# Fourteen expert rows of each head fetched and multiplied beside the next head's routing, with six score units a head

## The reference

```python
def peer_ffn(xn, w_query, sub_keys, expert_u, expert_v):
    q = (xt @ w_query).reshape(NT, PEER_HEADS, 2, D_KEY // 2)
    s = jnp.einsum('nhpd,pkd->nhpk', q, sub_keys)
    v1, i1 = lax.top_k(s[:, :, 0], PEER_TOPK)
    v2, i2 = lax.top_k(s[:, :, 1], PEER_TOPK)
    cand = (v1[..., :, None] + v2[..., None, :]).reshape(NT, PEER_HEADS, PEER_TOPK * PEER_TOPK)
    best, ci = lax.top_k(cand, PEER_TOPK)
    e1 = jnp.take_along_axis(i1, ci // PEER_TOPK, axis=-1)
    e2 = jnp.take_along_axis(i2, ci % PEER_TOPK, axis=-1)
    idx = e1 * N_KEYS + e2
    gate = jax.nn.softmax(best, axis=-1)
    ...
        act = jax.nn.gelu(jnp.einsum('cd,ced->ce', xc, expert_u[ic]), approximate=False)
        return jnp.einsum('ce,ced->cd', (gc * act).astype(xc.dtype), expert_v[ic])
```

## Time and profile before

| what | us |
| --- | --- |
| median of 3 runs | 4150.55 |
| lowest and highest | 4140.8, 4151.94 |
| the profiled execution's own time | 4146.39 |
| its span in the trace | 4144.7 |

### The profile page before, as it was taken

One profiled execution on the slowest core, in us unless ns is written; L12 is line 12 of the kernel. 1 busy time (PEld: TensorE's weight loads), 2 busy tenths in 40 slices (PEclk: granted clock), 3 DMA queues, 4 the chain that ended last, 5 costly groups with the idle time before them and its releaser, 6 DMA issues.

```text
span 4144.7 us, 68987 instructions
## 1 busy us (share of the span) xinstructions
PE 3987.2 (96%) x27233; PEld 3554.8 (86%) x27233; DVE 2572.6 (62%) x3495; ACT 1408.9 (34%) x1701; POOL 2311.4 (56%) x930
## 2 busy tenths in 40 slices
PE   7999999999999999989999889999999999999997
PEld 5777777777878787879999789999999999999997
DVE  4343344444455553167775677888738888888785
ACT  4323233333232221133333555555423223333223
POOL 4333233332333444444545457777768889999784
PEclk9999999999999999999999999999999999999998
DMA  3222222222132344233334579999989999999892
GB/s 125 90 85 80 90 75 89 86 85 93 70 117 87 130 143 145 98 130 136 125 124 149 209 281 391 398 398 410 386 321 395 373 383 398 397 390 400 313 383 102
DMA packets 258400, 899.46 MB, mean 217 GB/s; under 512 B 107672, under 2 KB 140696, under 8 KB 162736
## 3 DMA queue, kind: packets, MB, share of 16 engines
q1 hardware_dynamic: 175984, 482.50, 32.4%
q0 software_dynamic: 46080, 335.56, 19.7%
q10 hardware_dynamic: 36160, 78.85, 4.9%
HBM read 828.10 MB, written 68.71 MB: 216 GB/s over the span
## 4 chain that ended last, share of the span: by engine, by line
PE 66%; POOL 11%; issue 10%; DMA 6%; DVE 3%; ACT 3%; SPq 1%; ACTq 0%; POOLq 0%; DVEq 0%
PE ps L403 15%; PE ps L405 14%; PE ps L404 14%; PE ps L1990 5%; POOL wl L394 5%; PE ps L1992 5%; PE ps L1991 5%; DMA raw<-stream 5%; POOL wl L398 4%; PE ps L1679 2%; ACT wh L381 1%; POOL rowb L672 1%; ACT wh L390 1%; POOL act L678 1%; PE ps L1939 1%
## 5 line engine op out<-in xcount | busy, mean ns | idle before, releaser
L398 POOL TENSOR_TENSOR wl<-raw,wh 128x2048 fp32r<-128x2048 f32 x268 | 1245.3, 4647 | 1610.6 <-ACT wh L381 1610.5
L403 PE MATMUL ps<-xh,wh 128*128 128x352 f32 (+1 forms) x3904 | 1438.3, 368 | 37.4 <-DVE xl L1162 18.9
L405 PE MATMUL ps<-xh,wl 128*128 128x352 f32 (+1 forms) x3904 | 1403.8, 360 | 0.0
L404 PE MATMUL ps<-xl,wh 128*128 128x352 f32 (+1 forms) x3904 | 1402.3, 359 | 0.0
L403 PEld LDWEIGHTS ps<-xh,wh 128*128 128x128 f32 x3904 | 743.1, 190 | 136.8 <-issue 40.4
L405 PEld LDWEIGHTS ps<-xh,wl 128*128 128x128 f32 x3904 | 742.0, 190 | 83.0
L404 PEld LDWEIGHTS ps<-xl,wh 128*128 128x128 f32 x3904 | 743.1, 190 | 80.8 <-issue 7.7
L381 ACT ACTIVATE wh<-raw 128x2048 fp32r<-128x2048 f32 x270 | 516.8, 1914 | 859.1 <-PE ps L405 722.4
L1990 PE MATMUL ps<-gah,wh 128*128 128x352 f32 x2048 | 667.7, 326 | 33.5 <-POOL wl L394 22.7
L1992 PE MATMUL ps<-gah,wl 128*128 128x352 f32 x2048 | 662.5, 324 | 0.0
L1991 PE MATMUL ps<-gal,wh 128*128 128x352 f32 x2048 | 660.3, 322 | 0.0
(11 more groups left out here) (335 smaller groups left out, 4151.2 us busy)
## 6 DMA issues: line engine op xcount, KB each, us to landing
raw<-stream SPq DMA_DIRECT2D x396, 1024.0 KB, 5.1
gelu_scratch<-preb ACTq DMA_DIRECT2D x128, 176.0 KB, 6.0
gates_scratch<-stage ACTq DMA_DIRECT2D x22, 1024.0 KB
gt<-gates_scratch SPq DMA_DIRECT2D x32, 704.0 KB, 12.8
act<-gelu_scratch SPq DMA_DIRECT2D x32, 704.0 KB, 17.6
mergegate_scratch<-sgb ACTq DMA_DIRECT2D x32, 256.0 KB, 2.0
sgm<-mergegate_scratch SPq DMA_DIRECT2D x32, 256.0 KB, 2.7
h_in<-x_t SPq DMA_DIRECT2D x4, 1024.0 KB, 8.9
```

The lines of the kernel that those rows point to most:

```text
L398: pool.tensor_tensor(wl[s][:, :], raw[s][:, :], wh[s][:, :].bitcast(F32), ALU.subtract).then_inc(w_lo, 1)
L403: pe.matmul(dst, w_h, h[:, kx, lo:], start=start, stop=False)
L404: pe.matmul(dst, w_h, l[:, kx, lo:], start=False, stop=False)
L405: return pe.matmul(dst, w_l, h[:, kx, lo:], start=False, stop=stop)
```

## The change

SC_HEAD goes from 4 to 6, so 16 score units move from the gates' stage to the heads. Gates are then built in 28 units of two groups and 32 of one, 60 in all. Queries and key products all go through bank 7, so PE's order in a head is now query 0, score 0, query 1, score 1, keys 0, score 2, keys 1, scores 3 to 5. That leaves banks 0 to 3 for `xg` from the first head on: `turn` moves to head 0, and its input `xd` is computed ahead of the heads. The expert numbers of a head are computed as soon as its first token group has them (`sets_ready`). Of each of heads 0 to 6, fourteen rows are fetched by POOL in the next head's eight units, two behind each of seven of them, in four buffers, and used by DVE: six at the end of the head's own selection, four behind the next head's first-key selection, four behind its second-key selection. 30 rows of the first set stay in the gates' stage, behind unit 28. Of the second set 12 rows instead of 7 come before the border. ACT's exponential moves behind the second query unit. DVE's loop over heads is unrolled.

```diff
-SC_HEAD, SC_TAIL, SC_EGT, OH = 4, 6, 2, 4
+SC_HEAD, SC_TAIL, SC_EGT, OH = 6, 6, 2, 4
+SCORE_PLACE = (1, 3, 4, 5, 6, 7)
...
-GATES_TWO = 12
+GATES_TWO = 28
...
-fetches(0, 12, range(3, GATES_TWO), 0)
-fetches(12, SLOTS - 12, range(GATES_TWO, F_GATES + R_TURNED - 1), 0)
-fetches(SLOTS, 7, range(F_GATES + R_TURNED, J_BACK), F_GATES + R_TURNED + 1)
...
+EARLY = 14
+EARLY_ALL = EARLY * (HEADS - 1)
+EARLY_AT = {1: (0, 1), 2: (2, 3), 3: (4, 5), 4: (6, 7), 5: (8, 9), 6: (10, 11), 7: (12, 13)}
+EARLY_LAST, EARLY_KEYS, EARLY_VALUES = range(0, 6), range(6, 10), range(10, EARLY)
...
+MORE = 12
+FETCHED_AT.update({n: -1 for n in range(EARLY_ALL)})
+fetches(EARLY_ALL, SLOTS - EARLY_ALL, range(GATES_TWO, F_GATES + R_TURNED - 1), 0)
+fetches(SLOTS, MORE, range(F_GATES + R_TURNED, J_BACK), F_GATES + R_TURNED + 1)
...
+    homes = range(1, ROWS) if n < EARLY_ALL else range(ROWS_LOW if J_BACK <= FETCHED_AT[n] < J_HIGH else ROWS)
...
@@ gpsimd @@
+            for h in range(HEADS):
+                for c in range(PER_HEAD):
+                    split_lo(pool, U_QUERY + PER_HEAD * h + c, c % 2)
+                    for i in EARLY_AT.get(c, ()) if h else ():
+                        if i == 0:
+                            pool.wait_ge(sets_ready, h + 1)
+                        fetch(EARLY * (h - 1) + i)
...
@@ scalar, act_route @@
                 for c in range(2):
-                    act.wait_ge(w_used, n + c + 1)
-                    split_hi(act, n + c + 2, c)
+                    act.wait_ge(w_used, n + 2 * c + 1)
+                    split_hi(act, n + 2 * c + 2, 0)
                     if not first:
                         act.wait_ge(key_scores, 2 * h + c - 1)
-                    act.activation(qsb[:, c, :], bank(c), ACT.Copy).then_inc(q_saved, 1)
-                    if c == 0 and not first:
+                    act.activation(qsb[:, c, :], bank(7), ACT.Copy).then_inc(q_saved, 1)
+                    if c == 1 and not first:
                         act_softmax(h - 1)
+                    score(c)
...
@@ vector @@
+            dve.tensor_tensor(xd, xh[:, :, 0:P].bitcast(F32), xl[:, :, 0:P].bitcast(F32), ALU.add).then_inc(sets_ready, 1)
+            for h in range(HEADS):
...
+                    for i in (EARLY_VALUES if c else EARLY_KEYS) if h else ():
+                        use(EARLY * (h - 1) + i)
...
+                    if tt == 0:
+                        cut = slice(TOPK * h, TOPK * h + TOPK)
+                        own(dve, dve.scalar_tensor_tensor(idx[:, cut], EG[:, 0, 0, cut], float(NKEYS), EG[:, 1, 0, cut], ALU.mult, ALU.add), sets_ready, h + 2)
                 dve.wait_ge(ex_ready, h + 1)
...
+                for i in EARLY_LAST if h < HEADS - 1 else ():
+                    use(EARLY * h + i)
...
@@ tensor, head @@
+                if not first:
+                    pe.wait_ge(ssb_saved, 2 * h)
+                    unit(pe, n, 0, bank(7))
+                    score(0)
+                pe.wait_ge(q_saved, 2 * h + 1)
+                unit(pe, n + 2, 0, bank(7))
+                score(1)
+                if first:
+                    turn(1)
+                for c in range(2):
                     key_products(h, c)
-                    ahead(SC_HEAD * h + c, c, n + c, first)
-                for c in range(2, SC_HEAD):
-                    ahead(SC_HEAD * h + c, c % 2, n + c)
+                    score(2 + c)
+                for i in range(4, SC_HEAD):
+                    score(i)
```

More of the change, by code:

```diff
@@ L1415, in top16, with use @@
                 step(dve.max_index(idx[:, 8:16], vals[:, 8:16], rep))
-            with dve.Fori(0, HEADS) as h:
-                step.enter(h, 0, STEPS_ROUTE)
+            xg = ps[:, 0:4, :].rearrange("p b n -> p (b n)")
+            def use(n):
+                b = row_buffer(n)
+                dve.wait_ge(row_in[ROW_AT[n]], 16 * ROW_BEFORE[n] + 16)
+                if n < ALL:
+                    dve.scalar_tensor_tensor(b, b, 1.0, xg, ALU.mult, ALU.mult, accum_out=dots[:, slot(n):slot(n) + 1]).then_inc(row_used, 1)
+                else:
+                    dve.wait_ge(row_used, n)
+                    dve.scalar_tensor_tensor(xg, b, coef[:, slot(n):slot(n) + 1], xg, ALU.mult, ALU.add).then_inc(row_used, 1)
+            step(dve.tensor_copy(iota_route, iota128[:, :]))
+            for c in range(4):
+                dve.wait_ge(h_moved[c], 48)
+            dve.tensor_tensor(xd, xh[:, :, 0:P].bitcast(F32), xl[:, :, 0:P].bitcast(F32), ALU.add).then_inc(sets_ready, 1)
+            for h in range(HEADS):
                 for c in range(2):
@@ L1614, in first_units @@
                     for s in range(2):
-                        last = products(pe, bank(dst + s), s, k, P, xh, xl, k, k == 0, k == KT - 1)
+                        dst, lo = into[s]
+                        last = products(pe, dst, s, k, P, xh, xl, k, k == 0, k == KT - 1, lo)
                         if k == KT - 1:
@@ L1889, in key_products @@
             def key_products(h, c):
-                pe.wait_ge(q_saved, 2 * h + c + 1)
+                pe.wait_ge(q_saved, 2 * h + 2)
+                if c:
+                    pe.wait_ge(ssb_saved, 2 * h + 1)
                 for tt in range(TT):
-                    last = pe.matmul(bank(2 + c)[:, P * tt:P * tt + P], qsb[:, c, P * tt:P * tt + P], keys[:, c, :], start=True, stop=True)
+                    last = pe.matmul(bank(7)[:, P * tt:P * tt + P], qsb[:, c, P * tt:P * tt + P], keys[:, c, :], start=True, stop=True)
@@ L1893, in key_products, with turn, ahead @@
                 last.then_inc(key_scores, 1)
-            first_units(U_QUERY, 0, 1)
+            def turn(value):
+                pe.wait_ge(sets_ready, value)
+                for k in range(KT):
+                    last = pe.transpose(bank(k // 4)[:, P * (k % 4):P * (k % 4) + P], xd[:, k, :], ident[:, :])
+                last.then_inc(xg_ready, 1)
+            first_units(U_QUERY, ((bank(7), 0), (bank(4)[:, 0:N], G)), 1)
             pe.wait_ge(routing_in, 16)
-            def ahead(e, s, n, first=False):
+            def ahead(e, s, n, w=None, first=False):
@@ L1900, in ahead, with head @@
                 if not first:
                     pe.wait_ge(pre_ready, e - 1)
-                unit(pe, n, s, bank(4 + s)[:, 0:N], lo=G)
-            def head_scores(h, first=False):
-                n = U_QUERY + PER_HEAD * h + 2
+                unit(pe, n, s if w is None else w, bank(4 + s)[:, 0:N], lo=G)
+            def head(h, first=False):
+                n = U_QUERY + PER_HEAD * h
+                score = lambda i: ahead(SC_HEAD * h + i, i % 2, n + SCORE_PLACE[i], SCORE_PLACE[i] % 2, first and i < 2)
+                if not first:
[7 more added lines that the diff above has]
+                    turn(1)
@@ L1906, in head_scores @@
                 for c in range(2):
-                    if not first:
-                        pe.wait_ge(ssb_saved, 2 * h + c - 1)
                     key_products(h, c)
-                    ahead(SC_HEAD * h + c, c, n + c, first)
-                for c in range(2, SC_HEAD):
-                    ahead(SC_HEAD * h + c, c % 2, n + c)
-            head_scores(0, first=True)
+                    score(2 + c)
+                for i in range(4, SC_HEAD):
+                    score(i)
+            head(0, first=True)
@@ L1915, in _ @@
             with pe.Fori(1, HEADS) as h:
-                for c in range(2):
-                    unit(pe, U_QUERY + PER_HEAD * h + c, c, bank(c))
-                head_scores(h)
+                head(h)
             for e in range(SC_HEAD * HEADS, SC_HEAD * HEADS + SC_TAIL):
```

96 lines of the change are left out of this document (42 added, 54 removed).

## The result

The changed kernel takes **4384.4 us** in the median of four runs (4376.0 to 4385.6), the kernel before 4150.0 (4140.8 to 4151.9): ratio 1.0562, 95% interval 1.0537 to 1.0588, slower. The profiled execution's span is 4381.6 us (before 4144.7) and its mean granted clock 0.962 (0.984). The forecast was 4340, the range 4228 to 4400: the time came out 44 us above the forecast and inside the range.

The account below looks back on a forecast made before the run. PE, busy 96% of the span, was taken to bound the kernel. Sum: 4146.4 + 300.4 (heads) − 101.4 (gates) + 1.5 (handover) − 10 (late stages) = 4336.9, forecast 4340 us; range 4300 to 4400, with the DVE case 4228 to 4400.

Parts of the forecast that it names:

- The loop: Heads: waits through four engines, counted from D, DVE's first selection of head h−1; 97.5 us a head, +300.4 us; chance 0.78.
- Step 1: Heads, DVE: the expert numbers, behind eight products of the head before, are ready at D+58.5.
- Step 2: Heads, POOL: waits for the numbers, then two fetches and the second query's low half, done at D+65.5; PE idle 18 us.
- Step 3: Heads, PE: second query unit, 11.13 us plus 2 lost to the lowered clock after idling, done at D+78.7.
- Step 4: Heads, ACT: exponential only behind the second query, done at D+82.8; DVE's softmax, which waits for it, at D+83.8.
- Step 5: Heads, DVE: six products, 13.7 us, done at D+97.5; only then does DVE begin the next head.
- The gates' stage: Stage building the gates: 584.5 us instead of 685.9, so −101.4, at 11.4 us a two-group unit; bounds −108 and −86.
- the last rival: Gates' stage: two-group units fall to 8.6 us, another −73; total 4267 alone, 4090 if PE keeps its pace; chance 0.03.
- The late stages: Twelve units behind the gates and start of the values: −10 us of 10 and 9 lost there; bounds 0 and −19.
- DVE's length alone: Rival, heads: DVE runs without a gap at 82.1 us a head, +194.5 instead of +300.4; total 4235; chance 0.12.
- PE's pace: Rival, heads: the loop doesn't close, 70.2 us a head, +129; total 4150 to 4170; chance 0.07.
- the price from the Trainium skill: Heads: POOL's fetches drawn out beside DVE, 620 ns to about 3100; two add 4.3 us a head, estimate 4366.

Follow-up runs that it names:

- e1: The changed kernel with ACT's exponential of the head before behind the first query unit again instead of the second: 4318.7 us.
- e2: The changed kernel with a head's row fetches starting one unit later, behind the third unit's low half, the last four together behind the eighth: 4323.6 us.
- e3: The changed kernel without early rows, all 128 rows of the first set fetched and used in the gates' stage: 4253.9 us.
- e6: The changed kernel with ACT's rounding, GELU and scaling spread between its copies in the 28 two-group units: 4272.6 us.
- e4: The changed kernel with ACT's first copy from bank 6 ahead of rounding and GELU in the two-group units: 4350.2 us.
- e9: The changed kernel, fourteen rows kept, with the exponential behind the first query, fetches one unit later and ACT's work in two-group units spread: 4213.8 us.
- e7: The changed kernel with ACT's work in two-group units spread and six early rows a head instead of fourteen, fetched from unit 3 on: 4193.0 us.

## Why the prediction was right, and where it was off

**The loop (steps 1 to 5): right, nearly to the microsecond.** Step 1, numbers out: forecast D+58.5, measured D+58.4 (2013.88 to 2072.25). Step 2, POOL: D+65.5, measured 2079.41, D+65.5. Step 3, the query with 2 us lost to the clock: D+78.7, measured D+79.2 (2093.07); its first ten matmuls start 0.43 us apart at granted clock 0.50 (1.2 GHz; 2079.46 to 2083.90), the later ones 0.23 at 1.00, so the lower level lasted 4.4 us and cost 2. Step 4, exponential and softmax: D+83.8, measured D+84.0. Step 5, the products: D+97.5, measured D+97.8 in this head and 97.5 in the mean of the last six. D(0) was 1837.8 for 1837, D(1) 1917.0 for 1916.4, D(6) 2404.9 for 2403.9; the end of the tail 2580.2 for 2576.6. Two waits inside were off without moving the sum: PE reached the late weights at D+50.5 instead of D+47 and idled 15.1 us for 18, and DVE waited 16.4 us for the exponential instead of 13 to 15. e1 and e2 show it as cause: each opens one limb and takes 61 to 66 us, and e3, without rows, has no wait at all in the heads.

**The gates' stage: the mis-sized term.** Forecast 584.5 us, measured 616.3 (2601.2 to 3217.5). The first two units took 28.6 (27.3), the 32 with one group 260.6 (260.8), but the 26 others 12.58 each instead of 11.4: +31. I took one interval between two GELUs of before, 11.13, as the length of a unit without a row and put the excess of the mean, 12.7, on rows. It was neither typical nor quite without a row (POOL issues a fetch in it, at 2338.45; no product is made yet). The unit from 2309.04 to 2321.70, ahead of any fetch, had taken 12.66. What sets 11.13 apart is the clock, in the kernel before as in the changed one:

```profile
2333.54:2344.67 11.13, 8.92 (x57) 8.58 (x56) 6.14 (x10) 6.88 (x16) 5.53 (x2) 1.00 0.69 270
2369.59:2382.90 13.31, 10.95 (x60) 10.40 (x59) 8.44 (x13) 6.79 (x15) 5.50 (x2) 0.87 0.85 337
```

So the step that failed is the price of 11.4 a two-group unit: it put at nothing the lower clock that the waits bring, 1.5 us in each of 18 of the 26 units, 28 us in all, though the earlier trace rows shows 0.91 for this stage. Waits longer than the 2.2 us of the unit I chose add 10, and the 0.3 a unit that I had allowed covers 7 of the sum. The 12.7 that all units of before had in the mean came again in the changed kernel, with no row at all. My bound of 12 was too low by the same error, and two signs were missed by it: 616 us for 577 to 600, and the stage's end 237 us later instead of about 200. The cause I named in the last rival, ACT's rounding and GELU in front of its copy, was right for the waits, as e6 shows, and that rival's price was near (8.6; 8.9 measured). The rival itself did not come about: it needs another order in ACT's queue, which the change does not bring.

**The late stages**: −10 forecast, −0.4 measured. The twelve units gained 5 (99.2 for 104.3 us), the values to the end lost 4.7. That second stretch is 1058, 1064, 1062 and 1055 us long in e1, e2, e4 and e6, whose code is the same there, so its 4.7 can't be told from scatter. The handovers in front of the gates cost 1.4 us more than the 1.5 allowed. In all +3.6, +1.4, +31.8 and +9.6 make the 46 us between forecast and profiled execution. The gates' stage came out beyond its bounds and the late stages at the end of theirs; that the total stayed inside the range owes to the 41 us that the range kept for the heads, of which they needed 4. That part is luck.

**The rivals.** DVE's length alone (4235): its condition is met in e2 and e9, where POOL and ACT are in time, but its 82.1 us lacked 5 for the softmax step beside POOL. PE's pace (4150 to 4170): met in e3 and e7 in the heads, 70.3 us and the tail's end at 2406 for my 2405. The totals there (4253.9 and 4193.0) stayed above the rival's 4150 to 4170: the rows that leave the heads lengthen the units that take them, two-group units in e3 (13.9 us), one-group units in e7 (10.6). By the price from the Trainium skill the estimate was 4366, nearer to the total than my sum, but for a wrong reason: the fetches that it would lengthen kept their 0.94 us.
